# Merge, output projection and expert query of a hybrid encoder layer: sums kept in PSUM, squares added on VectorE, two query blocks interleaved

## What is computed

```python
def merge(gate_logits, y_gla, y_swa, y_mem, w_out):
    g1, g2, g3 = jnp.split(sigmoid(gate_logits), 3, axis=-1)
    return (g1 * y_gla + g2 * y_swa + g3 * y_mem) @ w_out
x += merge(...)                       # y_gla is (o * silu(r)) @ w_gla_o
h = rmsnorm(x, g_ffn)                 # over the 2048 features of a token
q = h @ w_peer_q                      # the first step of peer(h)
```

## Time and profile before

| what | value |
|---|---|
| median of 3 runs | 5248.3 us |
| the profiled execution, its own time | 5256.26 us |
| its span in the profile | 5254.4 us |
| mean granted TensorE clock, share of full | 0.977 |
| TensorE busy | 5013.3 us (95%) |
| VectorE, ScalarE, GpSimd busy | 3060.7, 1065.7, 3014.7 us |
| merge, first to last matmul | 2062.8 to 2266.6 us |
| output projection, first to last matmul of its blocks | 2281.6 to 2488.5 us |
| query, from the first matmul | 2498.2 us |

### The profile page before, as it was taken

How to read it: one execution, slowest core, us unless ns; L and a number is a source line. 1 busy time by engine, 2 the same in 40 slices (tenths; PEclk the granted TensorE clock), 3 DMA queues, 4 the chain that set the end, 5 groups by cost and what they waited for, 6 DMA issues and landing times. The chain is left out here.

```text
span 5254.4 us, 88668 instructions
## 1 busy us (share of the span) xinstructions
PE 5013.3 (95%) x32484; PEld 4873.4 (93%) x32484; DVE 3060.7 (58%) x4477; ACT 1065.7 (20%) x1535; POOL 3014.7 (57%) x1788
## 2 busy tenths in 40 slices
PE   7999999999998988989989999999998999999998
PEld 7999999899898777989989999999998999999998
DVE  4477777111112244520118877888885789888866
ACT  4133333233323342000101211111111000000001
POOL 7300000434343323545448777888886999999985
PEclk9999999999999998999999999999999999999999
DMA  6333333423233343542324446988887888888862
GB/s 249 112 128 128 125 125 120 135 79 105 100 122 134 113 170 138 186 148 83 126 101 140 137 137 215 331 328 327 323 322 256 301 309 310 300 311 308 303 209 105
DMA packets 344686, 1011.75 MB, mean 193 GB/s; under 512 B 39680, under 2 KB 133728, under 8 KB 308848
## 3 DMA queue, kind: packets, MB, share of 16 engines
q1 hardware_dynamic: 164960, 524.56, 29.6%
q0 software_dynamic: 36864, 268.45, 13.4%
q10 hardware_dynamic: 142640, 215.86, 11.6%
HBM read 883.11 MB, written 126.76 MB: 192 GB/s over the span
## 5 line engine op out<-in xcount | busy, mean ns | idle before, releaser
L218 POOL TENSOR_SCALAR w_hi<-w_raw 128x1024 fp32r<-128x1024 f32 x750 | 825.3, 1100 | 1983.3 <-PE ps L255 1064.5
L222 POOL TENSOR_TENSOR w_lo<-w_raw,w_hi 128x1024 fp32r<-128x1024 f32 x750 | 1854.9, 2473 | 140.2 <-POOL w_hi L218 135.8
L251 PE MATMUL ps<-h_hi,w_hi 128*128 128x272 f32 (+1 forms) x4768 | 1313.2, 322 | 83.9 <-PEq L1925 14.9
L255 PE MATMUL ps<-h_hi,w_lo 128*128 128x272 f32 (+1 forms) x4768 | 1291.4, 317 | 0.0
L253 PE MATMUL ps<-h_lo,w_hi 128*128 128x272 f32 (+1 forms) x4768 | 1284.2, 316 | 0.0
L251 PEld LDWEIGHTS ps<-h_hi,w_hi 128*128 128x128 f32 x4768 | 820.0, 190 | 109.5 <-issue 104.7
L253 PEld LDWEIGHTS ps<-h_lo,w_hi 128*128 128x128 f32 x4768 | 820.4, 190 | 5.8
L255 PEld LDWEIGHTS ps<-h_hi,w_lo 128*128 128x128 f32 x4768 | 816.1, 190 | 2.7
L251 PE MATMUL ps<-ex_c_hi,w_hi 128*128 128x416 f32 x2048 | 719.2, 351 | 21.7 <-DVE ex_c_lo L2723 21.7
L255 PE MATMUL ps<-ex_c_hi,w_lo 128*128 128x416 f32 x2048 | 724.2, 354 | 0.0
L253 PE MATMUL ps<-ex_c_lo,w_hi 128*128 128x416 f32 x2048 | 716.3, 350 | 0.0
(11 more groups left out here) (302 smaller groups left out, 7535.6 us busy)
## 6 DMA issues: line engine op xcount, KB each, us to landing
w_raw<-weights SPq DMA_DIRECT2D x906, 512.0 KB
up<-up_out ACTq DMA_DIRECT2D x128, 208.0 KB, 2.9
gate<-g_sb_g ACTq DMA_DIRECT2D x13, 2048.0 KB
ex_up<-up ACTq DMA_DIRECT2D x32, 832.0 KB
ex_gate<-gate ACTq DMA_DIRECT2D x32, 832.0 KB
proj<-in_stage ACTq DMA_DIRECT2D x73, 272.0 KB, 2.1
br_gate<-proj ACTq DMA_DIRECT2D x48, 272.0 KB, 3.8
mem_x_part<-x ACTq DMA_DIRECT2D x8, 1088.0 KB, 7.1
```

The lines of the kernel that those rows point to most:

```text
L218: pool.tensor_scalar(self.whi[:, slot, :], self.raw[:, slot, :], 1.0, 1.0, ALU.mult, ALU.mult).then_inc(self.hi_done, 1)
L222: pool.tensor_tensor(self.wlo[:, slot, :], self.raw[:, slot, :], self.whi[:, slot, :].bitcast(F32), ALU.subtract).then_inc(self.split_done, 1)
L251: pe.matmul(acc, hi, x, start=first, stop=False)
L255: mm = pe.matmul(acc, lo, x, start=False, stop=last)
```

## The change

In the merge stage the loops of ScalarE and VectorE are written out. The first five loads are issued at once; a load for j+1 is issued when VectorE is done with the buffer in block j. VectorE writes the first product into PSUM (accumulator 2 + j % 2), the second in place in SBUF, and adds them into `part`, ahead of the accumulator. The accumulator is multiplied by gate 0 and added to in place; ScalarE rounds from PSUM, VectorE subtracts from PSUM. TensorE waits for `rest` of block j-2, not for `y0`.

In the output projection the squares are added by VectorE into accumulator 2, one after each addition to x, the first with a copy; TensorE multiplies by ones only the sum of the first 15 (moved to SBUF, into `norm.tmp`) and the last square, after the last block. Its loop has 8 rounds of 2 blocks in place of 4 of 4.

In the query, blocks 0 and 1 are computed together: for each chunk both blocks' products. Two weight pieces change places in the host's array to fit that order.

```diff
@@ -1927,12 +1927,11 @@
         lo = ctx.enter_context(nc.sbuf_tensor("br_lo", [P, KD, T], F32R))
         gate = ctx.enter_context(nc.sbuf_tensor("br_gate", [P, 3, T], F32))
         other = ctx.enter_context(nc.sbuf_tensor("br_other", [P, 2, T], F32))
-        m = ctx.enter_context(nc.sbuf_tensor("br_m", [P, T], F32))
         part = ctx.enter_context(nc.sbuf_tensor("br_part", [P, 2, T], F32))
         load = SplitLoad(core, "br", hi, lo, io["gla_out"])
         loaded = [core.sem(f"br_terms_loaded{b}") for b in range(3)]
         split = core.sem("br_merged_hi")
-        dve_s = Steps(core.sem("br_dve"), ["y1", "y2", "y0", "sum1", "sum2", "rest"])
+        dve_s = Steps(core.sem("br_dve"), ["y1", "y2", "part", "y0", "sum", "rest"])
         block = ctx.enter_context(nc.Block())
 
         @block.sync
@@ -1950,7 +1949,7 @@
                 for u in range(2):
                     j = 2 * q + u
                     if needed(q):
-                        pe.wait_ge(dve_s.sem, dve_s.at("y0", j - 2))
+                        pe.wait_ge(dve_s.sem, dve_s.at("rest", j - 2))
                         held(pe)
                     for piece in range(2):
                         starts = isinstance(j, int) and j == 0
@@ -1962,57 +1961,46 @@
 
         @block.scalar
         def _(act):
+            def load_terms(j, b):
+                act.dma_start(gate[:, b, :], row(io["proj"], j + (B_GATE + KD * b))).then_inc(loaded[b], 16)
+                if b:
+                    act.dma_start(other[:, b - 1, :], row(io["branches"], j + KD * (b - 1))).then_inc(loaded[b], 16)
+
+            def load_next(j, b):
+                if j + 1 < KD:
+                    act.wait_ge(dve_s.sem, dve_s.at("part" if b == 2 else f"y{b}", j))
+                    load_terms(j + 1, b)
             load.scalar(act)
-
...
+            for b in (1, 2, 0):
+                load_terms(0, b)
+            for j in range(KD):
+                for b in (1, 2, 0):
+                    load_next(j, b)
+                act.wait_ge(dve_s.sem, dve_s.at("sum", j))
+                act.activation(halves_of(merged_hi[:, j, :]), core.acc_view(j % 2), ACT.Copy).then_inc(split, 1)
 
         @block.vector
         def _(dve):
             load.vector(dve)
-
...
+            for j in range(KD):
+                acc, y1, terms = core.acc_view(j % 2), core.acc_view(2 + j % 2), halves_of(part[:, j % 2, :])
+                if j >= 2:
+                    dve.wait_ge(dve_s.sem, dve_s.at("sum", j - 2))
+                dve.wait_ge(loaded[1], 32 * (j + 1))
+                dve.tensor_tensor(y1, halves_of(other[:, 0, :]), halves_of(gate[:, 1, :]),
+                                  ALU.mult).then_inc(*dve_s.did("y1"))
+                dve.wait_ge(loaded[2], 32 * (j + 1))
+                dve.tensor_tensor(other[:, 1, :], other[:, 1, :], gate[:, 2, :], ALU.mult).then_inc(*dve_s.did("y2"))
+                dve.wait_ge(dve_s.sem, dve_s.at("y2", j))
+                dve.tensor_tensor(terms, y1, halves_of(other[:, 1, :]), ALU.add).then_inc(*dve_s.did("part"))
+                dve.wait_ge(loaded[0], 16 * (j + 1))
+                dve.wait_ge(core.piece_used, 2 * j + (AT_GLA_OUT + 2))
+                dve.tensor_tensor(acc, acc, halves_of(gate[:, 0, :]), ALU.mult).then_inc(*dve_s.did("y0"))
+                dve.wait_ge(dve_s.sem, dve_s.at("y0", j))
+                dve.tensor_tensor(acc, acc, terms, ALU.add).then_inc(*dve_s.did("sum"))
+                dve.wait_ge(split, j + 1)
+                dve.tensor_tensor(halves_of(merged_lo[:, j, :]), acc, halves_of(merged_hi[:, j, :].bitcast(F32)),
+                                  ALU.subtract).then_inc(*dve_s.did("rest"))
 
 
 def stage_output_and_query(core, hi, lo):
@@ -2029,6 +2017,7 @@
         norm = Norm(core, ctx, "ffn", x, KD, T, G_FFN, hi, lo, 6, added, lambda k: k + 1)
         block = ctx.enter_context(nc.Block())
         rows = lambda name: io[name].rearrange("b p t -> p b t")
+        squares, squares_sum = core.acc_view(2), norm.tmp[:, 0, :]
 
         @block.sync
         def _(sp):
@@ -2039,40 +2028,72 @@
         def _(pool):
             core.split_pieces(pool, AT_OUT + RING, AT_UP + RING)
 
...
+        @block.tensor
+        def _(pe):
+            def out_blocks(q):
+                for u in range(2):
+                    b = 2 * q + u
+                    if needed(b - 1):
+                        pe.wait_ge(added, b - 1)
                     held(pe)
                     for piece in range(2):
-                        i = first_piece + 2 * u + piece
-
-                        starts = accs == 4 and isinstance(b, int) and b == 0
-                        core.use_piece(pe, i % RING, i + 8 * q, [
-                            (core.acc(u % accs), parts(hi, k), parts(lo, k), k == 0, k == KD - 1,
-                             (norm.lo_ready, k + 1) if starts else None, None)
+                        i = AT_OUT + 2 * u + piece
+                        core.use_piece(pe, i % RING, i + 4 * q, [
+                            (core.acc(u), parts(hi, k), parts(lo, k), k == 0, k == KD - 1)
                             for k in range(PIECE_K * piece, PIECE_K * (piece + 1))])
-                    between(q, u)
-            rounds(pe, KD // 4, body)
-
-        @block.tensor
-        def _(pe):
-            def square(q, u):
-
-                if isinstance(q, int) and q == 0 and u < 2:
-                    return
-                norm.add_square(pe, 4 * q + (u - 2), u % 2, isinstance(q, int) and q == 0 and u == 2, False)
-            blocks(pe, AT_OUT, 2, added, square)
-            for k in (KD - 2, KD - 1):
-                norm.add_square(pe, k, k % 2, False, k == KD - 1)
-            blocks(pe, AT_PQ, 4, out_ready, lambda q, u: None)
+            rounds(pe, KD // 2, out_blocks)
+            pe.wait_ge(norm.sq_used, KD - 1)
+            for out, (t0, n) in zip(norm.sum, norm.halves):
+                pe.matmul(out, core.ones, squares_sum[:, t0:t0 + n], start=True, stop=False)
+            pe.wait_ge(norm.sq_ready, KD)
+            for out, (t0, n) in zip(norm.sum, norm.halves):
+                mm = pe.matmul(out, core.ones, norm.sq[:, (KD - 1) % 2, t0:t0 + n], start=False, stop=True)
+            mm.then_inc(norm.sq_used, 1)
+
+            def both(piece):
+                for b in range(2):
+                    pe.wait_ge(core.split_done, AT_PQ + 2 * piece + b + 1)
+                for kk in range(PIECE_K):
+                    k = PIECE_K * piece + kk
+                    pe.wait_ge(norm.lo_ready, k + 1)
+                    for b in range(2):
+                        slot = (AT_PQ + 2 * piece + b) % RING
+                        w_hi = core.whi[:, slot, kk * P:(kk + 1) * P]
+                        w_lo = core.wlo[:, slot, kk * P:(kk + 1) * P]
+                        for acc, x_hi in zip(core.acc(b), parts(hi, k)):
+                            pe.matmul(acc, w_hi, x_hi, start=k == 0, stop=False)
+                        for acc, x_lo in zip(core.acc(b), parts(lo, k)):
+                            pe.matmul(acc, w_hi, x_lo, start=False, stop=False)
+                        for acc, x_hi in zip(core.acc(b), parts(hi, k)):
+                            mm = pe.matmul(acc, w_lo, x_hi, start=False, stop=k == KD - 1)
+                        if kk == PIECE_K - 1:
+                            mm.then_inc(core.piece_used, 1)
+
+            def query_block(b, u, i):
+                if needed(b - 3):
+                    pe.wait_ge(out_ready, b - 3)
+                held(pe)
+                for piece in range(2):
+                    core.use_piece(pe, (AT_PQ + 2 * u + piece) % RING, i + piece, [
+                        (core.acc(u), parts(hi, k), parts(lo, k), k == 0, k == KD - 1)
+                        for k in range(PIECE_K * piece, PIECE_K * (piece + 1))])
+            both(0)
+            both(1)
+            for b in range(2, 4):
+                query_block(b, b, AT_PQ + 2 * b)
+            with pe.Fori(1, KD // 4) as q:
+                for u in range(4):
+                    query_block(4 * q + u, u, 8 * q + (AT_PQ + 2 * u))
 
         @block.scalar
         def _(act):
-            norm.scalar(act)
+            for k in range(KD):
+                act.wait_ge(added, k + 1)
+                if k >= 2:
+                    act.wait_ge(norm.sq_used, k - 1)
+                act.activation(norm.sq[:, k % 2, :], x[:, k, :], ACT.Square).then_inc(norm.sq_ready, 1)
+            norm.root(act)
+            norm.copies(act)
 
             act.wait_ge(norm.lo_ready, KD)
             act.dma_start(rows("x2"), x[:, :, :]).then_inc(kept, 16)
@@ -2082,7 +2103,7 @@
                     b = 4 * q + u
                     if needed(16 * q):
                         act.wait_ge(stored[u], 16 * q)
-                    act.wait_ge(core.piece_used, AT_PQ + 2 * b + 2)
+                    act.wait_ge(core.piece_used, AT_PQ + 2 * b + (2 if needed(b - 1) else 3))
                     held(act)
```

(51 more changed lines are left out.)

15 lines of the change are left out of this document (removed).

## The result

The changed kernel takes 5213.2 us (median of 6 runs, 5206.8 to 5217.7), against 5249.8 us for the kernel before (6 runs, 5242.4 to 5255.4): ratio 0.9929, 95% interval 0.9919 to 0.9939. That is 36.7 us less, where 38.3 were forecast; 5210.0 stood against 5213.2, inside the range of 5202 to 5224. A second measurement gave 5213.4 us and a ratio of 0.9936 (0.9922 to 0.9950).

What follows compares the result with a forecast made beforehand. TensorE, busy 95% of the span, was taken as the bound, with time to gain where it waits or does movable work. Gains 8.7 + 10.4 + 0.6 + 10.9 + 7.7 = 38.3 us gave a median of 5210.0 us, range 5202 to 5224.

Steps and rivals of the forecast that it cites:

- Merge, inside: Merge blocks: with loads and products ahead of the accumulator, TensorE waits for nothing; gain 8.7 us, at least 6.9.
- Hole: Between merge and output projection: TensorE's standstill shrinks from 14.9 to 4.5 us, POOL's split ending last; gain 10.4 us.
- Clock: Start of the output projection: less half clock behind the shorter standstill; gain 0.6 us, bounds 0 and 2.6.
- Squares: Output projection: 14 squares leave TensorE, 11.8 us, less 0.9 for a later root; net 10.9 us.
- Query: Query's first two blocks computed together, VectorE slowed by two POOL splits in a row; gain 7.7 us.
- Later stages move as a whole: Stages after the query start after barriers, so they shift together; no term in the sum.
- rival 1: Merge to later stages: one hand-off shrinks less than computed; together a gain of 25 us, 5223 us; chance 0.12.
- rival 2: Clock holds through the short hole (+2.0 us) and TensorE bounds the query pair (+3.4): 5205 us; chance 0.07.
- PSUM (3): Merge and output projection: VectorE's and ScalarE's PSUM accesses hold TensorE's writes, 68 us; slower, 5278 us; chance 0.04.
- the change does nothing (4): Merge and query keep their waits, an unseen thing bounds the gap; only squares count, 10.9 us: 5237 us; chance 0.04.

Runs made afterwards that it cites:

- x4_sbuf_sums: Changed kernel with the merge's accumulator product and sum kept in SBUF instead of PSUM, loads still ahead: 5219.0 us, ratio 0.9946 to the kernel before.
- x2_squares: Kernel before with only the output projection's squares moved to VectorE, merge and query as before: 5243.0 us, ratio 0.9988.
- x5_pool_waits: Changed kernel, but POOL splits the query pair's two freed weight pieces only after VectorE's last lo: 5209.9 us, ratio 0.9929 to the kernel before.
- x6_psum: Changed kernel with 8 more VectorE additions reading and writing PSUM in each of 14 output blocks: 5212.8 us in one run.
- x7_warm: Changed kernel with unread matmuls in TensorE's idle time, 8 after the merge, 13 after the last square: 5209.2 us, ratio 0.9924 to the kernel before.
- x8_both: Changed kernel with POOL's splits held until the last lo and unread matmuls in TensorE's idle time: 5208.2 us, ratio 0.9926 to the kernel before.

## Why the prediction was right, point by point

*Merge, inside* (8.7 forecast): with the new stage the merge took 194.1 to 195.3 us in all eight profiles that have it; with the old one 203.9, 194.5, 202.4, 207.9 and 207.8, 203.3 on average against 194.7. So the gain is 8.6 on average, of which 1.2 are half clock at the stage's start and behind its waits. That the average comes so near to 8.7 is luck: the forecast read one execution, and the five give anything from 0 to 13 us. The mechanism was right, and its bound was not: "at least the 6.9 of the waits" was one execution's value, and a later one had none.

*Hole* (10.4, from 14.9 to 4.5): 4.45 us each time with the sums in PSUM. POOL's split ends it, as computed. The chain of VectorE was overestimated by 0.6 us, among it 0.25 from ScalarE's rounding to the subtraction, which start 0.66 us apart with PSUM as source, not 0.91. It didn't matter, since POOL was later anyway. The hole before was 12.8 to 15.5, so this gain too varies, between 8.4 and 11.0.

*Clock* (0.6): not earned. Behind the hole of 4.45 us the output projections of four profiles without extra matmuls took 195.2, 195.2, 194.2 and 194.2 us, x4_sbuf_sums behind 5.25 us 194.1, and x2_squares behind 15.5 us 194.5. With the clock held they took 192.7. So a short hole costs 1.5 to 2.5 us as a long one does. The half clock did not always begin in the hole: in x5_pool_waits and x6_psum the projection began at the upper level (1.00) and fell to 0.50 after 0.6 us, for 3.4 us.

*Squares* (11.8 less 0.9): outputs with squares on TensorE average 206.6 us (five profiles), without them 194.6 (six, those with extra matmuls left out): 12.0, less 0.7 for the root. The working counted one interval of 15 without squares; there are two, since the first square is multiplied at 2320.1, after the third block. The other 13 take (192.3 - 24.06) / 13 = 12.94, that is 0.91 us for a square and 11.9 for 13 of them, so the sum hardly changes.

*Query* (7.7): the pair from 36.95 to 29.20 us. The chain through two splits, taken instruction by instruction from one row of a blocked lo, gave 29.3. The query as a whole gained 8.1. The 0.4 more lie in its 14 other blocks, whose copies come 12.00 us apart, (2656.2 - 2500.2) / 13, where they came 12.03 apart before; no row shows why.

*Later stages move as a whole*: the rest took 2539.2 to 2546.4 us, with the change and without it. The first profile of the changed kernel had 2.9 us more than that of the kernel before, its second 0.5 less, so that difference was chance.

*Why 36.7 and not 38.3 in the medians.* The sum was made against one execution whose merge and hole were near the long end: its stretch was 651.6, and the mean of three is 647.0. Against that mean the changed kernel gains 34.1 us, and the two measurements gave 36.7 and 33.1 of medians. Against its own execution the sum was near, 38.3 for 38.7.

Of rival 1 nothing came: the pair gained what was forecast, no load of terms was late behind the first block, and the later stages didn't move. Of rival 2 neither half came by itself: the clock held only where x7_warm and x8_both made it, and TensorE bounded the pair only where POOL was made to wait. PSUM (3) was tested directly, with 10 accesses of VectorE to PSUM in an output block, where the merge's has 5 and one of ScalarE. That the change does nothing (4) is ruled out by every stretch.

## What to carry to other kernels

When an engine and a round trip beside it have almost the same period, one profile says little about what the round trip costs: look at several, or take the mean, before the term enters a sum. Find who is second at each barrier: here it was the engine that only splits weights, which ended 0.8 us after the main chain, so that making this chain shorter still would have gained nothing. And ask of an engine that gets free slots earlier what it will collide with: interleaving two blocks freed two pieces at once, and their splits took 3.1 us out of the very chain that the interleaving was to hide.

## What was not expected of the hardware

A merge with the same instructions took 194.5 us in one execution and 207.9 in another, with landing times of 4.2 and 4.7 us (medians of the same 32 loads). On the critical loop it is the last load of each block that counts: from the end of the rounding to its landing the two differ by 0.8 us on average, and that is 11 us over 14 blocks. And 3.8 us of useless matmuls in a hole of 4.45, the first of them right behind the last real one, kept the granted clock at 1.00; the idle time that was left was 0.80 us:

```profile
2248.35 3.83 PE L1963 MATMUL ps<-const_sb 128*128 128x272 f32 x16
2252.97 0.49 PE L251 MATMUL ps<-h_hi,w_hi 128*128 128x272 f32 x2 [0.80 <-PEq L1925]
```
